# Second-layer memory attention: f32 matmuls exchanged for three passes over high and low halves, with all of x copied to DRAM meanwhile

## The reference

```python
def mem_cross_attention(q_mem, mem_n, w_kv):
    B, S, _ = q_mem.shape
    kv = mem_n @ w_kv
    km, vm = split_cols(kv, [MEM_W, MEM_W])
    q = q_mem.reshape(B, S, N_MEM_HEADS, HEAD_DIM)      # 4 heads of 128
    km = km.reshape(B, -1, N_MEM_HEADS, HEAD_DIM)       # 256 memory tokens
    vm = vm.reshape(B, -1, N_MEM_HEADS, HEAD_DIM)
    s = jnp.einsum('bshd,bmhd->bhsm', q, km).astype(jnp.float32) / math.sqrt(HEAD_DIM)
    p = jax.nn.softmax(s, axis=-1).astype(vm.dtype)
    return jnp.einsum('bhsm,bmhd->bshd', p, vm).reshape(B, S, MEM_W)
```

## Time and profile before

| | |
|---|---|
| median of 3 runs | 1609.71 us |
| the profiled execution | 1609.3 us |
| its span | 1607.5 us |
| TensorE busy | 1586.2 us, 99% |
| VectorE busy | 993.7 us, 62% |
| ScalarE busy | 761.7 us, 47% |
| GpSimd busy | 623.6 us, 39% |
| granted TensorE clock | 0.999 of full speed |

### The profile page before, as it was taken

How to read it: one execution, slowest core, us unless ns; L and a number is a source line. 1 busy time by engine, 2 the same in 40 slices (tenths; PEclk the granted TensorE clock), 3 DMA queues, 4 the chain that set the end, 5 groups by cost and what they waited for, 6 DMA issues and landing times.

```text
span 1607.5 us, 21857 instructions
## 1 busy us (share of the span) xinstructions
PE 1586.2 (99%) x8856; PEld 1360.7 (85%) x8856; DVE 993.7 (62%) x1469; ACT 761.7 (47%) x1143; POOL 623.6 (39%) x309
## 2 busy tenths in 40 slices
PE   9999999999999999999999999999999999999998
PEld 6888898888888888888888777889878779999997
DVE  7787867676765365455553777682355785555554
ACT  7534344343432334555555464424435645554544
POOL 1002113221344334455555454353223215555552
PEclk9999999999999999999999999999999999999999
DMA  6454334343365413233324331122111223322321
GB/s 239 151 207 132 125 125 131 125 131 125 123 215 207 152 70 115 96 105 105 106 92 145 115 119 66 53 106 83 40 53 66 79 92 105 105 94 104 105 92 53
DMA packets 54412, 182.93 MB, mean 114 GB/s; under 512 B 6556, under 2 KB 7196, under 8 KB 53928
## 3 DMA queue, kind: packets, MB, share of 16 engines
q1 hardware_dynamic: 54312, 181.55, 32.9%
HBM read 174.42 MB, written 3.96 MB: 111 GB/s over the span
## 4 chain that ended last, share of the span: by engine, by line
PE 86%; DVE 9%; ACT 2%; issue 1%; POOL 1%; DMA 0%; SPq 0%; DVEq 0%; ACTq 0%; POOLq 0%
PE banks L468 84%; PE banks L471 2%; DVE wl L1259 1%; DVE TM L1828 1%; DVE ACC L1295 1%; DVE X L1228 1%; ACT T L2167 1%; POOL wl L2801 1%; DVE HL L1228 0%; DVE ada L1228 0%; ACT L2167 0%; DVE T L2059 0%; DVE TM L1836 0%; DMA X<-xT_dram 0%; DVE T L1228 0%
## 5 line engine op out<-in xcount | busy, mean ns | idle before, releaser
L2801 POOL TENSOR_TENSOR wl<-raw,wh 128x1024 fp32r<-128x1024 f32 x139 | 351.5, 2532 | 365.2 <-ACT wh L2170 365.2
L468 PE MATMUL banks<-HH,wh 128*128 128x512 f32 (+2 forms) x944 | 362.4, 386 | 4.4 <-ACT wh L2170 1.5
L468 PE MATMUL banks<-HL,wh 128*128 128x512 f32 (+2 forms) x944 | 353.0, 380 | 0.3 <-DVE HL L1228 0.3
L2170 ACT ACTIVATE wh<-raw 128x1024 fp32r<-128x1024 f32 x246 | 256.5, 1050 | 187.6 <-PE banks L468 180.4
L468 PE MATMUL banks<-HH,wl 128*128 128x512 f32 (+1 forms) x936 | 251.0, 380 | 1.4 <-POOL wl L2801 0.8
L468 PEld LDWEIGHTS banks<-HH,wh 128*128 128x128 f32 (+1 forms) x944 | 177.2, 188 | 43.3 <-issue 3.4
L468 PEld LDWEIGHTS banks<-HL,wh 128*128 128x128 f32 (+1 forms) x944 | 176.6, 188 | 35.7 <-DVE HL L1228 2.1
L468 PEld LDWEIGHTS banks<-HH,wl 128*128 128x128 f32 x936 | 172.1, 188 | 36.4 <-POOL wl L2801 2.1
L468 PE MATMUL banks<-wh,HH 128*128 128x256 f32 x448 | 127.7, 285 | 0.0
L468 PE MATMUL banks<-wl,HH 128*128 128x256 f32 x448 | 126.7, 283 | 0.0
L468 PE MATMUL banks<-wh,HL 128*128 128x256 f32 x448 | 126.6, 283 | 0.0
(11 more groups left out here) (429 smaller groups left out, 3306.9 us busy)
## 6 DMA issues: line engine op xcount, KB each, us to landing
raw<-wst_dram SPq DMA_DIRECT2D x294, 512.0 KB, 3.3
X<-xT_dram SPq DMA_DIRECT2D x8, 512.0 KB, 6.3
CB<-sums_dram SPq DMA_DIRECT2D x12, 256.0 KB, 3.1
D<-dec_dram SPq DMA_DIRECT2D x12, 256.0 KB, 2.8
out_dram<-XT SPq DMA_DIRECT2D x8, 256.0 KB
x_dram<-X SPq DMA_DIRECT2D x3, 512.0 KB, 6.1
QS<-QX SPq DMA_DIRECT2D x24, 64.0 KB, 2.5
KSw<-KX SPq DMA_DIRECT2D x24, 64.0 KB, 2.0
```

What stands on the lines that cost most here:

```text
L468: return pe.eng.matmul(dst, w, x, start=start, stop=stop, skip_group_check=True)
L2170: return eng.activation(dst, src, ACT.Copy)
L2801: tt(wl[:, q, :], raw[:, i % NRAW, :], wh[:, q, :].bitcast(F32), ALU.subtract).then_inc(*by_pool("low", u))
```

## The change

The halves get names and places:

- `KMH`, `KML` and `VMH`, `VML`: rounded keys and values of all four heads, and what is left of them. `KMH` and `VMH` lie where X was, the low halves replace the f32 keys and values in place.
- `QH`, `QL`: the queries' halves, the low one in place of `Qt`. `MPH`, `MPL`: the halves of the turned probabilities; `MPH` lies where `PT` was, `MPL` where X was, in part over its eighth feature tile.

Scores become 12 matmuls (Q high by K high and by K low, then Q low by K high), values 6. Keys and values are rounded once by ScalarE, before it splits the first weight tile that stands after `project_out(0)`, and subtracted once by GpSimd, the keys before its next tile split, the values two tiles later. Queries are rounded by ScalarE (`query_high`) and subtracted by VectorE right behind each `store_q` (`query_low`). Both halves of the turned probabilities are now copied by ScalarE, and VectorE subtracts both from the banks. `keep_x` and `bring_x` copy all eight feature tiles. Layer 0 stays as it is.

```diff
@@ -340,6 +340,11 @@
     PL, VL = at("PL", [128, 1152], 52, F32R), at("VL", [128, 3, 256], 57, F32R)
     sums = nc.dram_tensor("sums_dram", (12, T), F32, kind="Internal").ap()
 
+
+    KMH, KML = at("KMH", [128, 4, 256], 48, F32R), at("KML", [128, 4, 256], 156, F32R)
+    VMH, VML = at("VMH", [128, 2, T], 52, F32R), at("VML", [128, 2, T], 160, F32R)
+    MPH, MPL = at("MPH", [128, 1024], C0 + 21, F32R), at("MPL", [128, 1024], 56, F32R)
+
     RS = at("RS", [128, T], C0 + 2)
     QR, KR = at("QR", [128, T], C0), at("KR", [128, T], C0 + 4)
     PT2 = [PT, at("PTodd", [128, 1280], 156)]
@@ -627,6 +632,20 @@
                 tokens(("vm", l, j), MH, ML, 2, kh, (b,), feed.take(), lambda k: done("l", "mem", k))
 
         def mem_scores(l, h):
+            if l == 1:
+                pe.wait_ge(done("mq high", h), done("mk low"))
+                for i in range(4):
+                    o = bank[2 + i // 2][:, 256 * (i % 2):256 * (i % 2) + 256]
+                    pe.wait_ge(*free[2 + i // 2])
+                    mm(o, QH[:, h % 2, 128 * i:128 * i + 128], KMH[:, h, :], i % 2 == 0, False)
+                    mm(o, QH[:, h % 2, 128 * i:128 * i + 128], KML[:, h, :], False, False)
+                pe.wait_ge(done("mq low", h))
+                for i in range(4):
+                    o = bank[2 + i // 2][:, 256 * (i % 2):256 * (i % 2) + 256]
+                    mm(o, QL[:, h % 2, 128 * i:128 * i + 128], KMH[:, h, :], False, i % 2 == 1).then_inc(*by_pe("m scored", l, h, i))
+                for i in range(2):
+                    free[2 + i] = (done("m exp", l, h, 2 * i + 1),)
+                return
             pe.wait_ge(done("q", ("qm", 2 * l + h // 2), h % 2), done("kept", ("km", l, h // 2), 0))
             for i in range(4):
                 b = 2 + i // 2
@@ -647,6 +666,19 @@
                 free[b] = (done("m pt", l, h, j),)
 
         def mem_attend(l, h):
+            if l == 1:
+                c = slice(128 * h, 128 * h + 128)
+                pe.wait_ge(done("mv low"), *free[5])
+                for j in range(2):
+                    pe.wait_ge(done("m ph", h, j))
+                    mm(bank[5], VMH[:, j, c], MPH[:, T * j:T * j + T], j == 0, False)
+                    mm(bank[5], VML[:, j, c], MPH[:, T * j:T * j + T], False, False)
+                for j in range(2):
+                    pe.wait_ge(done("m pt", l, h, j))
+                    e = mm(bank[5], VMH[:, j, c], MPL[:, T * j:T * j + T], False, j == 1)
+                e.then_inc(*by_pe("m out", l, h))
+                free[5] = (done("z used", l, 12 + h),)
+                return
             pe.wait_ge(done("kept", ("vm", l, h // 2), 0), *free[5])
             for j in range(2):
                 pe.wait_ge(done("m pt", l, h, j))
@@ -1346,6 +1378,12 @@
             mem_end(l, h)
 
         def mem_turn(l, h):
+            if l == 1:
+                for j in range(2):
+                    dve.wait_ge(done("m ph", h, j), done("x kept", 3), now["pt read"])
+                    tt(MPL[:, T * j:T * j + T], bank[(4, 7)[j]], MPH[:, T * j:T * j + T].bitcast(F32),
+                       ALU.subtract).then_inc(*by_dve("m pt", l, h, j))
+                return
             dve.wait_ge(done("m turned", l, h, 1), now["pt read"])
             eng.tensor_copy(PT[:, T:2 * T], bank[7]).then_inc(*by_dve("m pt", l, h, 1))
 
@@ -1551,10 +1589,16 @@
 
         project_out(0, {(0, 0): [lambda: fox_turn(11)], (0, 1): [lambda: fox_attend(11)]})
 
+        def query_low(h):
+            j = h % 2
+            dve.wait_ge(done("mq high", h), done("q", ("qm", 2 + h // 2), j))
+            tt(QL[:, j, :], Qt[:, j, :], QH[:, j, :].bitcast(F32), ALU.subtract).then_inc(*by_dve("mq low", h))
+
         feed.unit()
         now["q read"] = None
         for j in range(2):
             store_q(("qm", 2), j, RS, "x1")
+            query_low(0 + j)
         mem_scores(1, 0)
         feed.unit()
         for j in range(2):
@@ -1568,6 +1612,7 @@
         feed.unit(lambda: mem_attend(1, 0))
         for j in range(2):
             store_q(("qm", 3), j, RS, "x1")
+            query_low(2 + j)
         mem_turn(1, 1)
         mem_scores(1, 2)
         feed.unit(lambda: mem_attend(1, 1))
@@ -2236,6 +2281,12 @@
             now["sm free"] = done("m recip", l, h)
 
         def mem_turn(l, h):
+            if l == 1:
+                for j in range(2):
+                    act.wait_ge(done("m turned", l, h, j), now["pt read"])
+                    copy(MPH[:, T * j:T * j + T], bank[(4, 7)[j]]).then_inc(*by_act("m ph", h, j))
+                now["s read"] = done("m turned", l, h, 1)
+                return
             act.wait_ge(done("m turned", l, h, 0), now["pt read"])
             copy(PT[:, 0:T], bank[4]).then_inc(*by_act("m pt", l, h, 0))
             now["s read"] = done("m turned", l, h, 1)
@@ -2377,7 +2428,18 @@
 
         project_out(0, {(0, 0): [lambda: fox_turn(11)], (0, 1): [lambda: fox_attend(11)]})
 
+        def query_high(h):
+            j = h % 2
+            act.wait_ge(done("q", ("qm", 2 + h // 2), j), done("x kept", 0))
+            copy(QH[:, j, :], Qt[:, j, :]).then_inc(*by_act("mq high", h))
+
+        act.wait_ge(done("x kept", 1), done("kept", ("km", 1, 1), 0), done("l", "x1", 3))
+        copy(KMH[:, :, :], km[1][:, :, :]).then_inc(*by_act("mk high"))
+        act.wait_ge(done("x kept", 2), done("kept", ("vm", 1, 1), 0), done("l", "x1", 5))
+        copy(VMH[:, :, :], vm[1][:, :, :]).then_inc(*by_act("mv high"))
         feed.unit(lambda: scales("x1", T, RS[:, :], 2, done("unit", ("out", 0, 3), 1)))
+        for h in range(2):
+            query_high(h)
         mem_begin(1, 0)
         feed.unit()
         for j in range(2):
@@ -2385,6 +2447,8 @@
         mem_turn(1, 0)
         mem_begin(1, 1)
         feed.unit(lambda: mem_attend(1, 0))
+        for h in range(2, 4):
+            query_high(h)
         mem_turn(1, 1)
         mem_begin(1, 2)
         feed.unit(lambda: mem_attend(1, 1))
@@ -2859,7 +2923,12 @@
             feed.take()
             if i == 1:
                 finish(0, 11)
-        units(2)
+        pool.wait_ge(done("mk high"), done("kept", ("km", 1, 1), 0))
+        tt(KML[:, :, :], km[1][:, :, :], KMH[:, :, :].bitcast(F32), ALU.subtract).then_inc(*by_pool("mk low"))
+        feed.unit()
+        pool.wait_ge(done("mv high"), done("kept", ("vm", 1, 1), 0))
+        tt(VML[:, :, :], vm[1][:, :, :], VMH[:, :, :].bitcast(F32), ALU.subtract).then_inc(*by_pool("mv low"))
+        feed.unit()
         feed.unit(lambda: finish(1, 12))
         feed.unit(lambda: finish(1, 13))
         finish(1, 14)
@@ -3018,14 +3087,12 @@
         for i in range(2):
             dma(X[:, 2 * i:2 * i + 2, :], a["xT"][:, 2 * i:2 * i + 2, :]).then_inc(*x_in[i]("x again", i))
         def keep_x(i):
-            n = 2 if i < 3 else 1
-            sp.wait_ge(done("kept", ("out", 0, i), n - 1))
-            dma(kept_x[:, 2 * i:2 * i + n, :], X[:, 2 * i:2 * i + n, :]).then_inc(*x_out[i]("x kept", i))
+            sp.wait_ge(done("kept", ("out", 0, i), 1))
+            dma(kept_x[:, 2 * i:2 * i + 2, :], X[:, 2 * i:2 * i + 2, :]).then_inc(*x_out[i]("x kept", i))
 
         def bring_x(i):
-            n = 2 if i < 3 else 1
             sp.wait_ge(done("x kept", i))
-            dma(X[:, 2 * i:2 * i + n, :], kept_x[:, 2 * i:2 * i + n, :]).then_inc(*x_in[i]("x back", i))
+            dma(X[:, 2 * i:2 * i + 2, :], kept_x[:, 2 * i:2 * i + 2, :]).then_inc(*x_in[i]("x back", i))
 
         for n in range(16):
             feed.take()
```

## The result

The changed kernel takes **1612.01 us**, median of 16 runs (1611.62 to 1613.70). The kernel before, run beside it, takes 1609.12 (16 runs, 1608.83 to 1609.77). The ratio is 1.0019, 95% interval 1.0012 to 1.0026: the change makes the kernel 2.9 us slower. The forecast was 1611.1 us with a range of 1607.0 to 1612.5, and the result lies inside it. The profiled execution took 1611.6 us with a span of 1609.8; the one before 1609.3 and 1607.5.

A forecast was written before the change was run, and what follows sets the result against it. TensorE, 99% busy at full clock, was taken to bound the kernel. A saving of 1.8 us against two waits of 1.8 us gave +1.75 us on 1609.3: forecast 1611.1 us, range 1607.0 to 1612.5.

The forecast's parts named there:

- What bounds the kernel: Whole kernel: TensorE, busy 99% of the span at 2.4 GHz, so time changes only where it does less or waits.
- The passes: Second layer's memory heads: scores save 0.21 us and values 0.34 a head, 2.2 us over four heads (1.3 to 2.6).
- the short waits: Copies right in front of the values of heads 2 and 3: 0.38 us altogether, leaving 1.8 us saved.
- Once-only work: Rounding and low halves of keys and values, and larger copies of x: hidden, costing nothing.
- VectorE beside GpSimd: Memory heads: VectorE operations with two SBUF inputs, the added query_low among them, stand still while GpSimd works.
- The two waits: TensorE waits 1.8 us in head 2's scores for VectorE's QL, and 1.8 us before its values for ScalarE.
- Behind it the distances between engines are those of before: After memory head 3: nothing more gained or lost.
- The sum: Whole kernel: -1.8 + 1.8 + 1.8 = +1.75 us on the profiled 1609.3, forecast 1611.1 us.
- 1 (saving kept): Rival: low halves do not wait or fall in gaps, passes' saving stays: -2.0, 1607.3 us; chance 0.22.
- 2 (QL 2 first): Rival: QL 2 precedes tile 8, first wait vanishes, head 2's gate still late: +0.7, 1610.0 us; chance 0.14.
- 3: Rival: GpSimd does not let QL 0 in between, TensorE waits 2.4 us in head 0: +3.4, 1612.7 us; chance 0.10.
- 4: Rival: passes behind waits cost more, 0.9 us on the forecast, 1612.0 us; chance 0.54 together with the forecast.

The follow-up runs named there:

- experiment 5: The changed kernel with only the values in three passes and the scores in f32 as before: 1608.50 us, ratio 0.9995.
- experiment 3: Changed kernel; head 2's queries rounded before weight tile 8, QL of heads 1 and 3 made behind the minima of heads 0 and 2: 1608.78 us, ratio 0.9995.
- experiment 4: The kernel before with only the full copies of x, the last one 512 KB and not 256: 1609.29 us, ratio 1.0000.
- experiments 9 to 12: Warm-up matmuls: 24 more in the kernel before (1610.88 us), the changed kernel (1613.47) and experiment 3 (1610.30); ten fewer in experiment 5 (1608.17).
- experiment 2: The changed kernel with ScalarE rounding the queries of head 2 ahead of splitting weight tile 8: 1611.80 us, ratio 1.0013.
- experiment 8: The kernel before with VectorE copying the second half of head 2's probabilities three times more: 1611.73 us, ratio 1.0012.
- experiment 12: Experiment 5 with ten warm-up matmuls fewer, 8 for 18: 1608.17 us, ratio 0.9993.
- experiment 11: Experiment 3 with 24 more matmuls in the warm-up: 1610.30 us, ratio 1.0006.

## Why the prediction was right, and where not

- **What bounds the kernel: right.** Every difference that was traced is TensorE's: work saved, a wait, or its clock.
- **The passes: right.** Scores 1.54 us for 1.52 forecast. Values: four of them alone gained 1.38 us over the stretch (experiment 5) against 1.36. In experiment 3, with the long waits gone, the whole saving is 1.8 us, the figure that the prediction has left after the short waits.
- **Once-only work: right.** The x copies cost nothing (experiment 4), and no wait answers to the keys' and values' halves.
- **VectorE beside GpSimd: right.** QL took 2.03, 1.51, 2.74, 0.69 us against 2.0, 1.6, 2.8, 0.7. The Trainium skill's rule (SBUF — State Buffer, "Who interferes with whom") agrees with these rows. In them VectorE ends 0.54 to 0.56 us behind GpSimd, though its operation takes 0.69 alone, and the one GpSimd operation that stood right behind took 2.84 us for 2.40.
- **The two waits: right in place and releaser, forecast somewhat too long.** 1.45 us for 1.8 in the scores of head 2, 1.67 for 1.8 before its values. QL 2 came 0.16 us after tile 8's start (0.19 forecast); it ended 0.56 us earlier than laid out (591.24 for 591.80), and TensorE wanted it 0.30 earlier (589.85 for 590.15), hence the smaller wait. Experiment 3 shows that both hang on the order of the added low halves: with it changed the one is gone and the other 0.18 us. Stretch as a whole: 1.14 + 0.24 = +1.38 against +1.75.
- **"Behind it the distances between engines are those of before": this step failed.** 1.15 us more went in the retention heads. The prediction put this term at nothing. It named what would show it, a wait anywhere later meaning a missed queue; the queue is that of TensorE's own instructions. I counted the DMAs that the change issues and not that the program, 24 records longer, fetches its instructions at other moments. The Trainium skill describes these fetches (Runtime: NRT & Kernel Launch, "Instruction fetch mechanics": blocks of 256 instructions, the cost of a boundary "mostly hidden"). The spacing agrees: 2 x 8,856 / 256 = 69.2, and the page of the profile before counts 69 of them. From TensorE itself they are hidden: in the kernel before it has no wait between 640 and 850 us, with ten fetches there. From the swaps, for which the critical path waits, they are not: experiments 9 to 12 and the 70 heads show it.
- **The sum.** -0.24 at the start, +1.38 in the stretch and +1.16 in the retention heads give 2.30, the difference of the profiled executions. Against the forecast of 1611.1, the stretch was put 0.37 too dear, 1.16 were missed and 0.24 were there before the stretch began: 0.55 us net for the profiled execution. That two misses of opposite sign partly cancel is luck: had the stretch cost what was forecast, the median would be 1612.4, past the forecast's own range (to 1612.2), though still inside the stated one. The other 0.4 us are the median's distance from the profiled execution, which lies at the low end of the 16 runs. Four of these took 1613.0 us or more, three of the four at a mean granted clock of 0.998, which none of the other twelve (1611.6 to 1612.5) shows. A clock at half for 3.4 us, as in experiment 2, would cost that much and lower the mean by 0.001; since no run above 1613 was profiled, it is an argument and not shown.
- **Rivals.** 1 (saving kept) is what experiment 3 turns the kernel into, -1.8 by the retention heads. 2 (QL 2 first) is experiment 2: the wait for QL went as it said, and the clock took the gain back. 3 did not come, QL 0 ends at 560.81. 4 did not: the passes cost what was taken.

What stays open: by what path one 16 KB packet (0.9 to 2.2 us, one DMA engine's time) delays the swaps by up to 1.3 us, even when it comes 2.5 us ahead of their first packet, and when the clock falls behind a wait and when not.

## To carry to other kernels

Where TensorE is 99% busy, half a microsecond saved per head is worth what the order of the added helper operations allows: put the low-half subtraction that nobody wants yet behind the operation that the chain of the next head waits for, and start it where GpSimd is idle. Lay the queues out before building: QL of head 2 was ready 0.16 us too late to go ahead of GpSimd's tile, and that made a wait of 1.45 us. And when a change makes TensorE's program longer or shorter, look at where its instruction fetches fall beside small DMAs on the critical path, before explaining a loss far from the edit; a few warm-up matmuls more or fewer test it.

## What the runs showed of the hardware

- Instruction fetches: 16 KB packets in queue 8, one per 128 matmul records with their weight loads (69 for 8,856), 0.9 to 2.2 us each. One packet of 1.25 us makes up 2.0% of what 16 DMA engines have in 4 us, so it keeps one of them busy. Near a pair of SBUF-to-SBUF swaps (eight DMAs of 64 KB) they lengthen these from at most 4.00 to at least 4.09 and up to 5.31 us (70 heads, fourteen kernels), and TensorE lost 0.18 to 1.41 us each time. Twenty-four more matmuls in the warm-up at the start of the program, which took no longer for them, cost 1.5 us of the median; the profile shows 0.9 us, lost over 600 us later.
- The granted clock fell to 0.50 for 3.4 us behind a TensorE wait of 1.9 us in experiment 2, and did not behind waits of 1.67 us (changed kernel) and 1.5 us (experiment 8). It was at half, too, after 2.84 us of idleness in experiment 12, and not after 1.48 us in experiment 11.
